# RMS-norm statistics of a three-block transformer kernel: row sums on four columns, and a scale spread back by one matmul

## The chip, the cores and the metric

One core of one Trainium2 chip runs the whole kernel as one launch. The time is device time in microseconds (us), the median of several runs. Engines are named as in the profile: PE (TensorE), ACT (ScalarE), DVE (VectorE), POOL (GpSimd), SP (SyncE, which only issues transfers here).

## The reference

512 tokens of 1024 features pass through three blocks, float32 throughout, with mixers of several kinds between the norms. What the change touches is the norm that stands ahead of every mixer and every feed-forward, 11 times on the main path:

```python
def rms_norm(t, w):
    tf = t.astype(jnp.float32)
    y = tf * lax.rsqrt(jnp.mean(tf * tf, axis=-1, keepdims=True) + NORM_EPS)
    return (y * w.astype(jnp.float32)).astype(t.dtype)

def modulate(h, shift, scale):
    return h * (1.0 + scale[:, None, :]) + shift[:, None, :]
```

The norm is followed by a product with a weight matrix. In the blocks where the kernel splits float32 operands into a rounded part ("hi") and a rest ("lo"), that product is hi·hi + hi·lo + lo·hi in the fp32r type.

## The kernel before

**Layout.** Features lie on the 128 partitions, tokens along the free axis: the residual `X(k)` and the norm's output `H(k)` are eight tiles, k = 0..7, of 128 x 512. A sum over features is therefore a sum over partitions and over the eight tiles.

**Order.** Each engine runs one program written out by hand, and they meet only through semaphores. A PE stage fills PSUM banks of a ring of four (`proj` for projections, `mix` for everything else); a key's place in the list of `mixing_keys` gives its bank. `Steps.done` makes an engine wait for its own instruction before it goes on.

**A norm.** `norm(r)`, r = 0..10, exists once for each engine. ACT squares X(k) into scratch tiles (`squares_at(r)`), each as soon as the residual of tile k is there. PE sums them with a 128x128 matrix of ones in `sum_squares` (L771), eight float32 products of 512 columns, which leaves the sum of each token on all partitions. ACT takes the root of the 128x512 result (`root`), DVE its reciprocal (`inverse`, L1682), and DVE then writes H(k) from X(k) and this factor. In the norms of `MODULATED` (0, 1, 2, 3, 9, 10) DVE multiplies by the factor only, and ACT applies gain and shift in one Identity over H(k). In those of `PLAIN` (4 to 8) DVE applies gain and factor in one instruction (L1656) and no shift exists. In `SPLIT_NORMS` ACT then rounds H(k) to hi (`round_h`), and DVE makes lo from H(k) and hi, after it has written all eight H(k).

**What follows.** Norms 1, 2, 3, 4, 5, 7 and 10 (`SPLIT_UP`) are followed by `first_pair`: PE makes two output tiles t = 0, 1 at once, for each k four products with hi of the norm (L683, L684) and, after all k, the products with lo (L689), first all of t = 0, then all of t = 1. The first two chunks of the next weight matrix are rounded by ACT (`round_chunk`) and DVE (`rest_chunk`) inside the norm. Chunk 2 goes into the buffer of chunk 0, so ACT rounds it when tile t = 0 is complete. Norm 9 is followed by projections of the context (`ck`, L648, then `cv`, L762) that don't use it, then by `rk`.

**What goes ahead.** `NORM_AFTER` names the stage ahead of norms 1 to 8. Where that is one of the four feed-forward down projections (`dn0` to `dn3`), the stage's own weight chunks, three for each output tile, are rounded by ACT in `round_down`, which stands ahead of `norm(r)`, and DVE makes their rest in `residual`. Norm 10 comes after `post_norm`, norm 0 first of all, after DVE has reduced the first rows of the modulation matrix.

Of the kernel before, what the change touches and what calls it, by code (L numbers as in the profile page):

```python
# [19 lines left out]
F32 = mybir.dt.float32  # L20
F32R = mybir.dt.float32r
I32 = mybir.dt.int32
ALU = mybir.AluOpType
# [186 lines left out]
def mixing_keys():  # L210

    k = [("ss", 0)]
# [16 lines left out]
    k += [("ss", 1), ("ss", 2)]  # L229
# [5 lines left out]
    k += [("ss", 3), ("ss", 4)]  # L235
# [6 lines left out]
    k += [("ss", 5), ("ss", 6), *(("dw", t) for t in range(KD)), ("lnm", 0), ("lnv", 0), ("ss", 7), ("ss", 8), ("ssc", 0), ("ss", 9)]  # L242
# [5 lines left out]
    k += [("ssy", 0), ("ss", 10), ("ssy", 1)]  # L248
# [29 lines left out]
class Chip:  # L278


    def __init__(self, nc, ctx, dram):
# [26 lines left out]
        self.small = sb("small", [P, 160])  # L308
# [10 lines left out]
        with ExitStack() as mlstm:  # L319
# [19 lines left out]
            "cond_ready", "pos_ready", "trig_ready", "ada_used", "ada_copied", "ada_first", "mod_ready", "sq_ready", "xn_ready", "h_ready",  # L339
# [138 lines left out]
PLAIN = {4: ("norm_mix_2", 0), 5: ("norm_ffn_2", 0), 6: ("norm_mix_2", 8), 7: ("norm_ffn_2", 8), 8: ("norm_final_2", 0)}  # L478
SQ0, RSTD = 44, 54

# [147 lines left out]
def tensor_program(nc, pe, c):  # L628
# [44 lines left out]
    def first_pair(name, r, lo):  # L673
# [100 lines left out]
    def norm(r):  # L774
        sum_squares(("ss", r), lambda k: (s["sq_ready"], 8 * r + k + 1), lambda k: T(squares_at(r) + k), KD)
# [366 lines left out]
def scalar_program(nc, act, c):  # L1142
# [17 lines left out]
    def round_h(r, k):  # L1160

        n = 8 * SPLIT_NORMS.index(r) + k + 1
        act.wait_ge(s["h_raw"], n)
        st.done(f(c.norm_hi(r, k), H(k), ACT.Copy), s["h_rounded"])
# [19 lines left out]
    def round_down(layer):  # L1184

        for n in range(SPLIT_RING, 3 * KD):
            round_chunk(f"dn{layer}", n)

    def norm(r):

        for k in range(KD):
            if r == 0:
                act.wait_ge(s["x_loaded"], 16)
            elif r in NORM_AFTER:
                act.wait_ge(*proj.emptied((NORM_AFTER[r], k)))
            else:
                act.wait_ge(s["x_ready"], 8 * (r - 9) + k + 1)
            st.done(f(T(squares_at(r) + k), X(k), ACT.Square), s["sq_ready"])
            if r in SPLIT_UP and k == KD - 2:

                up = SPLIT_UP[r]
                for n in range(SPLIT_RING):
                    round_chunk(up, n)
        root(("ss", r), T(RSTD), D)
        if r in MODULATED:
            use, layer, part, ready = MODULATED[r]
            act.wait_ge(s["mod_ready"], ready)
            for k in range(KD):
                act.wait_ge(s["xn_ready"], 8 * list(MODULATED).index(r) + k + 1)
                ins = f(H(k), H(k), ACT.Identity, scale=c.g(use, k), bias=c.m(layer, part, k))  # L1210
                ins.then_inc(s["h_raw"] if r in SPLIT_NORMS else s["h_ready"], 1)
                if r in SPLIT_NORMS:
                    round_h(r, k)
# [96 lines left out]
    def swiglu(layer):  # L1310
# [12 lines left out]
        round_down(layer)  # L1323
# [106 lines left out]
    def conv_ffn(layer):  # L1430
# [21 lines left out]
        round_down(layer)  # L1452
# [189 lines left out]
def vector_program(nc, dve, c):  # L1642
# [40 lines left out]

    def norm(r):
        if r in SPLIT_UP:
            for n in range(SPLIT_RING):
                rest_chunk(SPLIT_UP[r], n)
        inverse(("ss", r), T(RSTD))
        for k in range(KD):
            if r in MODULATED:  # L1690
                st.done(tt(H(k), X(k), T(RSTD), ALU.mult), s["xn_ready"])
            else:
                name, at = PLAIN[r]
                out = X(k) if r == 8 else H(k)
                ins = stt(out, X(k), c.v(name, at + k), T(RSTD), ALU.mult, ALU.mult)
                if r == 8:
                    st.done(ins, s["x_ready"])
                elif r in SPLIT_NORMS:
                    ins.then_inc(s["h_raw"], 1)
                else:  # L1700
                    ins.then_inc(s["h_ready"], 1)
                    dve.wait_ge(s["h_ready"], h_count(r, k))
        if r in SPLIT_NORMS:
            for k in range(KD):
                dve.wait_ge(s["h_rounded"], 8 * SPLIT_NORMS.index(r) + k + 1)
                tt(c.norm_lo(r, k), H(k), c.norm_hi(r, k).bitcast(F32), ALU.subtract).then_inc(s["h_ready"], 1)
# [23 lines left out]
    def residual(stage, gate=None, bias=None):  # L1730

        for k in range(KD):
# [670 lines left out]
```

## Time and profile before

| | us |
|---|---|
| median of 3 runs (lowest to highest) | 3945.15 (3940.18 to 3945.87) |
| the profiled execution's own time | 3940.18 |
| its span | 3938.5 |
| PE busy | 3498.3 (89% of the span) |
| DVE busy | 1952.3 (50%) |
| ACT busy | 1136.8 (29%) |
| mean granted PE clock | 0.942 |

PE is the busiest engine, but its idle time is what the other engines can shorten. In the rows below, times are us from the span's start; what stands in brackets at the end of a row is how long the engine sat idle ahead of it, and who ended that.

### The profile page before, as it was taken

The numbers are of one execution on the slowest core, as the hardware profiler recorded it, in microseconds if no ns is written. First come the engines' busy times: TensorE is split into PE (matmuls) and PEld (weight loads), VectorE is DVE, ScalarE is ACT, GpSimd is POOL, SyncE is SP. The second block draws the span as 40 slices with busy tenths as digits, with TensorE's granted clock in tenths as the row PEclk, the third lists the DMA queues.
The fourth block names the chain that finished last, engine by engine and source line by source line (L and its number), as shares of the span: only waits on it lengthen the run. The fifth ranks groups of instructions, "written<-read, shape, count | busy, mean of one in ns | idle before, by whom it ended". The sixth has DMA issues, their size and how long they took to land. (4 is left out here: it accounts for less than half of the span.)

```text
span 3938.5 us, 36809 instructions
## 1 busy us (share of the span) xinstructions
PE 3498.3 (89%) x12950; PEld 2448.4 (62%) x12950; DVE 1952.3 (50%) x2639; ACT 1136.8 (29%) x1457; POOL 111.8 (3%) x204
## 2 busy tenths in 40 slices
PE   4998789998689999965999999899997959998998
PEld 1444368886448877732588844378875725746886
DVE  5757255626438854334466259366523342316523
ACT  1211233324522213321344210244324222213221
POOL 0000000100000000000000030000000000000000
PEclk9897899999899999977999999899998979999999
DMA  5332146632025532300233311123332202222332
GB/s 210 103 117 70 32 133 192 194 118 64 22 64 193 191 121 84 94 11 7 79 95 99 93 53 54 38 86 97 95 112 75 86 11 74 86 69 75 96 97 73
DMA packets 100410, 360.90 MB, mean 92 GB/s; under 512 B 11152, under 2 KB 11168, under 8 KB 100064
## 3 DMA queue, kind: packets, MB, share of 16 engines
q1 hardware_dynamic: 77936, 276.07, 22.8%
q0 software_dynamic: 20080, 75.27, 6.0%
q10 hardware_dynamic: 2304, 8.39, 0.5%
q8 instruction: 53, 0.87, 0.1%
q14 instruction: 37, 0.30, 0.0%
HBM read 357.59 MB, written 2.10 MB: 91 GB/s over the span
## 5 line engine op out<-in xcount | busy, mean ns | idle before, releaser
L1648 DVE TENSOR_TENSOR weight_lo<-weight_ring,weight_hi 128x1024 fp32r<-128x1024 f32 (+1 forms) x422 | 508.0, 1206 | 1019.5 <-ACT weight_hi L1147 1015.5
L1147 ACT ACTIVATE weight_hi<-weight_ring 128x1024 fp32r<-128x1024 f32 (+1 forms) x422 | 440.2, 1044 | 1396.6 <-PE proj_banks L711 1058.1
L711 PE MATMUL proj_banks<-h_lo,weight_hi 128*128 128x512 f32 x1584 | 616.7, 389 | 0.0
L711 PE MATMUL proj_banks<-h_hi,weight_hi 128*128 128x512 f32 x1344 | 523.8, 390 | 8.8 <-DVE weight_lo L1648 8.8
L711 PE MATMUL proj_banks<-h_hi,weight_lo 128*128 128x512 f32 x1344 | 523.6, 390 | 0.0
L711 PEld LDWEIGHTS proj_banks<-h_lo,weight_hi 128*128 128x128 f32 x1584 | 297.8, 188 | 62.1
L711 PEld LDWEIGHTS proj_banks<-h_hi,weight_hi 128*128 128x128 f32 x1344 | 252.7, 188 | 62.3 <-issue 10.4
L711 PEld LDWEIGHTS proj_banks<-h_hi,weight_lo 128*128 128x128 f32 x1344 | 252.6, 188 | 52.7
L711 PE MATMUL proj_banks<-mid_hi,weight_hi 128*128 128x512 f32 x704 | 275.4, 391 | 7.3 <-DVE weight_lo L1648 7.3
L648 PE MATMUL proj_banks<-h_tiles,weight_ring 128*128 128x512 f32 x592 | 264.5, 605 | 13.8 <-ACT h_tiles L1147 7.3
L711 PE MATMUL proj_banks<-mid_lo,weight_hi 128*128 128x512 f32 x704 | 274.9, 390 | 0.0
L711 PE MATMUL proj_banks<-mid_hi,weight_lo 128*128 128x512 f32 x704 | 274.8, 390 | 0.0
L1147 ACT ACT_TABLE_LOAD x125 | 160.4, 1283 | 349.5 <-PE proj_banks L711 109.7
L668 PE MATMUL proj_banks<-h_tiles,weight_ring 128*128 128x512 f32 x512 | 225.7, 603 | 17.4 <-ACT h_tiles L1147 10.0
L1682 DVE RECIPROCAL scratch<-scratch 128x512 f32<-128x512 f32 (+1 forms) x39 | 129.2, 3312 | 218.7 <-ACT scratch L1147 218.6
L771 PE MATMUL mix_banks<-scratch,squares 128*128 128x512 f32 (+1 forms) x256 | 130.6, 664 | 113.8 <-ACT scratch L1147 109.2
L648 PEld LDWEIGHTS proj_banks<-h_tiles,weight_ring 128*128 128x128 f32 x592 | 114.9, 195 | 160.8 <-issue 158.2
L668 PEld LDWEIGHTS proj_banks<-h_tiles,weight_ring 128*128 128x128 f32 x512 | 98.9, 194 | 143.7 <-issue 141.9
L1147 ACT ACTIVATE scratch<-proj_banks 128x512 f32<-128x512 f32 (+1 forms) x186 | 105.0, 575 | 271.7 <-PE proj_banks L648 119.9
L1656 DVE SCALAR_TENSOR_TENSOR scratch<-proj_banks,vectors,scratch 128x511 f32<-128x511 f32 (+3 forms) x208 | 155.3, 747 | 26.8 <-ACT scratch L1147 13.3
L771 PEld LDWEIGHTS mix_banks<-scratch,squares 128*128 128x128 f32 x256 | 54.6, 220 | 180.8 <-issue 159.4
L1648 DVE TENSOR_TENSOR scratch<-scratch 128x512 f32<-128x512 f32 (+7 forms) x171 | 120.4, 704 | 87.0 <-ACT scratch L1147 45.4
(299 smaller groups left out, 5055.7 us busy)
## 6 DMA issues: line engine op xcount, KB each, us to landing
weight_ring<-in_w_up SPq DMA_DIRECT2D x176, 512.0 KB, 3.7
ada_ring<-in_ada POOLq DMA_DIRECT2D x96, 512.0 KB, 4.0
weight_ring<-in_w_dn SPq DMA_DIRECT2D x64, 512.0 KB, 3.5
weight_ring<-in_w_br SPq DMA_DIRECT2D x32, 512.0 KB, 3.7
weight_ring<-in_w_upr SPq DMA_DIRECT2D x32, 512.0 KB, 3.6
weight_ring<-in_w_dnr SPq DMA_DIRECT2D x32, 512.0 KB, 3.6
scratch<-in_ada POOLq DMA_DIRECT2D x24, 512.0 KB, 4.3
weight_ring<-in_w_dn SPq DMA_DIRECT2D x32, 384.0 KB, 3.2
```

The costliest lines, as they stand in the source:

```text
L648: last = mm(bank[:, 0:n], c.slot(chunk)[:, i * P:(i + 1) * P], rhs(k), start=k == 0, stop=k == sum(per) - 1)
L668: last = mm(proj.banks[:, u % RING, :], c.slot(ch)[:, n * P:(n + 1) * P], rhs(k), start=k == 0, stop=k == kt - 1)
L711: last = mm(proj.banks[:, u % RING, :], stationary(split0 + n)[:, w], moving(k), start=k + m == 0, stop=k == kt - 1 and m == 2)
L771: last = mm(bank[:, 0:n], c.square("ones"), tile(k), start=k == 0, stop=k == count - 1)
L1147: return nc.scalar.activation(out, in_, func, **kw)
L1648: return v.tensor_tensor(out, a, b, op)
L1656: return v.scalar_tensor_tensor(out=out, in0=a, scalar=x, in1=b, op0=op0, op1=op1)
L1682: st.link(v.reciprocal(rt, rt))
```

## The change

- **Statistics.** DVE adds squares 1 to 6 to square 0 (`sum_up`), one 128x512 add each; behind a `NORM_AFTER` stage this is spread over `residual`, otherwise it stands at the start of `norm`. PE then takes the squares as the stationary operand, four blocks of 128 tokens, against 16 columns of ones: four small products for the sum of squares 0 to 6, four more for square 7. The sum of each token now lies on its own partition, in four columns (`sum of block j` at column 16·j).
- **Root and reciprocal** are taken on 128x4. An extra 128x1 Sqrt on ACT after square 6 stands ahead of them.
- **Spread.** DVE multiplies the identity matrix by the four columns (four diagonal blocks, 128x512), and one product of ones with them puts the factor on all partitions, in a new bank ("bc", r), which stays in PSUM and is read from there.
- **Scale folded.** In the modulated norms DVE writes X·gain·factor, and ACT adds the shift while it rounds to hi; lo is made from H, shift and hi in one DVE instruction. H itself then lacks the shift.
- **Order.** `round_down` is gone: the chunks of a down projection are rounded between the squares of the norm that follows. Chunk 1 of the next stage is rounded after the root, and its rest comes after the diagonal. In `first_pair` the lo products run with k outside and t inside.

```diff
+STD, INV = 160, 164
+SUMS = 16
@@ PE
-        for t in range(2):
-            for k in range(KD):
-                if t == 0:
-                    pe.wait_ge(s["h_ready"], h_count(r, k))
+        for k in range(KD):
+            pe.wait_ge(s["h_ready"], h_count(r, k))
+            for t in range(2):
                 last = mm(proj.bank((name, t)), c.hi(split0 + t)[:, k * P:(k + 1) * P], lo(k), start=False, stop=k == KD - 1)
-            last.then_inc(proj.full_sem, 1)
+                if k == KD - 1:
+                    last.then_inc(proj.full_sem, 1)
...
     def norm(r):
-        sum_squares(("ss", r), lambda k: (s["sq_ready"], 8 * r + k + 1), lambda k: T(squares_at(r) + k), KD)
+        bank = open_bank(mix, ("ss", r))
+        for half, (sem, n) in enumerate(((s["sq_summed"], 6 * (r + 1)), (s["sq_ready"], 8 * (r + 1)))):
+            pe.wait_ge(sem, n)
+            for j in range(NB):
+                squares = T(squares_at(r) + (KD - 1 if half else 0))
+                last = mm(bank[:, j * SUMS:(j + 1) * SUMS], squares[:, j * P:(j + 1) * P], c.square("ones")[:, 0:SUMS], start=half + j == 0, stop=half + j == NB,
+                          skip_group_check=True)
+        last.then_inc(mix.full_sem, 1)
+        bank = open_bank(mix, ("bc", r))
+        pe.wait_ge(s["rstd_ready"], r + 1)
+        mm(bank, c.square("ones"), T(RSTD), start=True, stop=True).then_inc(mix.full_sem, 1)
@@ ACT, norm(r)
-                act.wait_ge(*proj.emptied((NORM_AFTER[r], k)))
+                stage = NORM_AFTER[r]
+                if stage in SPLIT:
+                    for n in range(3 * k + SPLIT_RING, min(3 * k + 3 + SPLIT_RING, 3 * KD - 1)):
+                        round_chunk(stage, n)
+                act.wait_ge(*proj.emptied((stage, k)))
...
-            if r in SPLIT_UP and k == KD - 2:
-                up = SPLIT_UP[r]
-                for n in range(SPLIT_RING):
-                    round_chunk(up, n)
-        root(("ss", r), T(RSTD), D)
+            if k == KD - 2:
+                st.link(f(c.small[:, STD:STD + 1], eps, ACT.Sqrt))
+                if NORM_AFTER.get(r) in SPLIT:
+                    round_chunk(NORM_AFTER[r], 3 * KD - 1)
+                if r in SPLIT_UP:
+                    round_chunk(SPLIT_UP[r], 0)
+        act.wait_ge(*mix.filled(("ss", r)))
+        ins = f(c.small[:, STD:STD + NB], mix.bank(("ss", r))[:, 0:NB * SUMS:SUMS], ACT.Sqrt, scale=1.0 / D, bias=eps)
+        ins.then_inc(mix.emptied(("ss", r))[0], 1)
+        if r in SPLIT_UP:
+            round_chunk(SPLIT_UP[r], 1)
...
-                ins = f(H(k), H(k), ACT.Identity, scale=c.g(use, k), bias=c.m(layer, part, k))
-                ins.then_inc(s["h_raw"] if r in SPLIT_NORMS else s["h_ready"], 1)
                 if r in SPLIT_NORMS:
-                    round_h(r, k)
+                    st.done(f(c.norm_hi(r, k), H(k), ACT.Identity, bias=c.m(layer, part, k)), s["h_rounded"])
+                else:
+                    f(H(k), H(k), ACT.Identity, bias=c.m(layer, part, k)).then_inc(s["h_ready"], 1)
@@ DVE
+    def sum_up(r, k):
+        total = T(squares_at(r))
+        dve.wait_ge(s["sq_ready"], 8 * r + k + 1)
+        st.done(tt(total, total, T(squares_at(r) + k), ALU.add), s["sq_summed"])
+
     def norm(r):
+        if r not in NORM_AFTER:
+            for k in range(1, KD - 1):
+                sum_up(r, k)
         if r in SPLIT_UP:
-            for n in range(SPLIT_RING):
-                rest_chunk(SPLIT_UP[r], n)
-        inverse(("ss", r), T(RSTD))
+            rest_chunk(SPLIT_UP[r], 0)
+        dve.wait_ge(*mix.emptied(("ss", r)))
+        st.link(v.reciprocal(small[:, INV:INV + NB], small[:, STD:STD + NB]))
+        st.done(tt(T(RSTD).rearrange("p (n c) -> p n c", c=P), c.square("ident").unsqueeze(1).broadcast_to([P, NB, P]),
+                   small[:, INV:INV + NB].unsqueeze(2).broadcast_to([P, NB, P]), ALU.mult), s["rstd_ready"])
+        if r in SPLIT_UP:
+            rest_chunk(SPLIT_UP[r], 1)
+        dve.wait_ge(*mix.filled(("bc", r)))
+        rstd = mix.bank(("bc", r))
         for k in range(KD):
             if r in MODULATED:
-                st.done(tt(H(k), X(k), T(RSTD), ALU.mult), s["xn_ready"])
+                ins = stt(H(k), X(k), c.g(MODULATED[r][0], k), rstd, ALU.mult, ALU.mult)
+                st.done(ins, s["xn_ready"])
...
@@ DVE, residual(stage), ahead of the wait for PE's tile k
+            if k >= 2:
+                sum_up(after, k - 1)
```

The order of instructions shows it at two places. First PE, norm 1 (behind the projection `abo`, ahead of the first pair of `up0`). Before:

```order
L668 MATMUL proj_banks<-h_tiles,weight_ring 128x512 x7
L657 REGISTER_ALU
L657 COMPARE_AND_BRANCH
L771 MATMUL mix_banks<-scratch,squares 128x512 [waits sq_ready,mix_empty2]
L771 MATMUL mix_banks<-scratch,squares 128x512 [waits sq_ready] x7
L683 MATMUL proj_banks<-h_hi,weight_hi 128x512 [waits w_split,proj_empty2,h_rounded]
```

And now:

```order
L674 MATMUL proj_banks<-h_tiles,weight_ring 128x512 x7
L663 REGISTER_ALU
L663 COMPARE_AND_BRANCH
L787 MATMUL mix_banks<-squares,scratch 128x16 [waits sq_summed,mix_empty3]
L787 MATMUL mix_banks<-squares,scratch 128x16 x3
L787 MATMUL mix_banks<-squares,scratch 128x16 [waits sq_ready]
L787 MATMUL mix_banks<-squares,scratch 128x16 x3
L792 MATMUL mix_banks<-scratch,squares 128x512 [waits rstd_ready,mix_empty0]
L689 MATMUL proj_banks<-h_hi,weight_hi 128x512 [waits w_split,proj_empty2,h_rounded]
```

Eight wide products have become eight narrow ones and one wide one, and that one waits for DVE's diagonal. ("squares" in these names is also the tensor that holds the constant square matrices, ones and identity among them; the squared tiles are in "scratch".)

Second DVE at the same norm, from the last residual on. Before:

```order
L1656 SCALAR_TENSOR_TENSOR x_tiles<-proj_banks,mod,x_tiles 128x512 [waits proj_full,proj_empty0]
L1648 TENSOR_TENSOR weight_lo<-weight_ring,weight_hi 128x1024 [waits w_rounded,proj_empty1]
L1648 TENSOR_TENSOR weight_lo<-weight_ring,weight_hi 128x1024 [waits w_rounded]
L1682 RECIPROCAL scratch<-scratch 128x512 [waits mix_empty2]
L1648 TENSOR_TENSOR h_tiles<-x_tiles,scratch 128x512 [waits dve_chain]
L1648 TENSOR_TENSOR h_tiles<-x_tiles,scratch 128x512 [waits xn_ready] x7
L1648 TENSOR_TENSOR h_lo<-h_tiles,h_hi 128x512 [waits h_rounded,xn_ready]
```

And now:

```order
L1667 TENSOR_TENSOR scratch<-scratch 128x512 [waits sq_ready,proj_empty0]
L1675 SCALAR_TENSOR_TENSOR x_tiles<-proj_banks,mod,x_tiles 128x512 [waits proj_full,sq_summed]
L1667 TENSOR_TENSOR weight_lo<-weight_ring,weight_hi 128x1024 [waits w_rounded,proj_empty1]
L1716 RECIPROCAL small<-small 128x4 [waits mix_empty3]
L1667 TENSOR_TENSOR scratch<-squares,small 128x512 [waits dve_chain]
L1667 TENSOR_TENSOR weight_lo<-weight_ring,weight_hi 128x1024 [waits w_rounded,rstd_ready]
L1675 SCALAR_TENSOR_TENSOR h_tiles<-x_tiles,gain,mix_banks 128x512 [waits mix_full]
L1675 SCALAR_TENSOR_TENSOR h_tiles<-x_tiles,gain,mix_banks 128x512 [waits xn_ready] x7
L1675 SCALAR_TENSOR_TENSOR h_lo<-h_tiles,mod,h_hi 128x512 [waits xn_ready,h_rounded]
```

An add of squares stands ahead of each residual, the wide reciprocal is a narrow one with the diagonal behind it, and the rest of chunk 1 lies between the diagonal and the first H(k).

## Rows read from the trace of the kernel before

**Rows 1.** Timeline around norm 1: start, us, engine, line, operation, tiles, count

```profile
508.39 7.03 PE L771 MATMUL mix_banks<-scratch,squares 128*128 128x512 f32 x16
508.66 0.75 DVE L1656 SCALAR_TENSOR_TENSOR x_tiles<-proj_banks,mod,x_tiles 128x512 f32<-128x512 f32 x1 [6.12 <-PE proj_banks L668]
509.45 0.63 ACT L1147 ACTIVATE scratch<-x_tiles 128x512 f32<-128x512 f32 x1 [4.14 <-DVE x_tiles L1656]
...
515.50 1.28 ACT L1147 ACT_TABLE_LOAD   x1 [5.42 <-PE mix_banks L771]
...
517.52 3.35 DVE L1682 RECIPROCAL scratch<-scratch 128x512 f32<-128x512 f32 x1 [5.71 <-ACT scratch L1147]
...
523.25 0.79 PE L683 MATMUL proj_banks<-h_hi,weight_hi 128*128 128x512 f32 x1 [7.82 <-ACT h_hi L1147]
...
534.88 3.82 PE L689 MATMUL proj_banks<-h_lo,weight_hi 128*128 128x512 f32 x16
...
540.75 0.47 PE L711 MATMUL proj_banks<-h_hi,weight_hi 128*128 128x512 f32 x1 [2.05 <-DVE weight_lo L1648]
```

**Rows 2.** Timeline, first product behind norms 4, 5, 6; norm 4's lo products

```profile
1551.40 0.80 PE L683 MATMUL proj_banks<-h_hi,weight_hi 128*128 128x512 f32 x1 [7.01 <-ACT h_hi L1147]
...
1560.19 3.79 PE L689 MATMUL proj_banks<-m_lo,weight_hi 128*128 128x512 f32 x16
...
1922.83 0.79 PE L683 MATMUL proj_banks<-h_hi,weight_hi 128*128 128x512 f32 x1 [5.73 <-ACT h_hi L1147]
...
2299.49 6.13 PE L648 MATMUL proj_banks<-h_tiles,weight_ring 128*128 128x512 f32 x7 [6.47 <-DVE h_tiles L1656]
```

**Rows 3.** Groups by line, and the instructions on the tensor small

```profile
L811 PE MATMUL proj_banks<-small_weights,h_tiles 128*128 128x8 f32 x64 | 11.5, 324 | 0.0
L1648 DVE TENSOR_TENSOR scratch<-scratch 128x512 f32<-128x512 f32 x130 | 90.0, 692 | 72.0 <-ACT small L1147 32.3 <-ACT scratch L1147 31.5
L1147 ACT ACTIVATE small<-small,others x2: 300/304/308, 2969.3 to 3158.2; 128x8 f32<-128x8 f32 x1, 128x16 f32<-128x16 f32 x1
```

**Rows 4.** One wide product with ones: in the chain that ended last, and the timeline

```profile
3555.97 1.14 PE mix_banks L771 x2
374.74 2.07 PE L883 MATMUL mix_banks<-scratch,squares 128*128 128x512 f32 x2
```

**Rows 5.** Windows, attention stretch: us, busy of each engine (instructions), PEclk

```profile
392.00:424.00 32.00, 15.36 (x48) 9.98 (x48) 12.55 (x46) 10.96 (x34) 0.00 (x0) 0.50 0.00 0
```

**Rows 6.** Timeline behind the first pair of norm 3

```profile
1177.70 0.47 PE L711 MATMUL proj_banks<-h_hi,weight_hi 128*128 128x512 f32 x1 [2.67 <-DVE weight_lo L1648]
```

**Rows 7.** Timeline in dn0, tile 6: residual, and rounding of the last chunk

```profile
877.34 0.75 DVE L1656 SCALAR_TENSOR_TENSOR x_tiles<-proj_banks,mod,x_tiles 128x512 f32<-128x512 f32 x1
...
880.55 0.85 ACT L1147 ACTIVATE weight_hi<-weight_ring 128x768 fp32r<-128x768 f32 x1 [4.38 <-PE proj_banks L711]
```

**Rows 8.** Timeline around norm 0

```profile
59.55 0.17 DVE L1656 SCALAR_TENSOR_TENSOR gain<-mod,vectors 128x8 f32<-128x8 f32 x1
...
67.72 2.90 PE L648 MATMUL proj_banks<-h_tiles,weight_ring 128*128 128x512 f32 x3 [7.32 <-ACT h_tiles L1147]
```

**Rows 9.** Timeline around norm 9, PE: sum of squares, ck, cv

```profile
2970.45 9.03 PE L771 MATMUL mix_banks<-scratch,squares 128*128 128x512 f32 x16 [12.21 <-ACT scratch L1147]
2979.31 13.98 PE L648 MATMUL proj_banks<-scratch,weight_ring 128*128 128x256 f32 x64
2998.43 4.83 PE L762 MATMUL proj_banks<-weight_ring,scratch 128*128 128x512 f32 x7 [5.14 <-ACT scratch L1147]
```

**Rows 10.** Timeline around norm 10, and its first pair

```profile
3553.46 0.69 DVE L1648 TENSOR_TENSOR x_tiles<-x_tiles,scratch 128x512 f32<-128x512 f32 x1
...
3563.64 0.79 PE L683 MATMUL proj_banks<-late_rounded,weight_hi 128*128 128x512 f32 x1 [6.54 <-ACT late_rounded L1147]
...
3575.25 3.79 PE L689 MATMUL proj_banks<-h_lo,weight_hi 128*128 128x512 f32 x16
...
3579.82 0.47 PE L711 MATMUL proj_banks<-late_rounded,weight_hi 128*128 128x512 f32 x1 [0.77 <-DVE weight_lo L1648]
```

More of the change, by code:

```diff
@@ L210, in mixing_keys @@
 def mixing_keys():
-    k = [("ss", 0)]
+    k = [("ss", 0), ("bc", 0)]
     k += [("rot_i", t) for t in range(5)]
@@ L234, in mixing_keys @@
         k += [("sb", h - 2)] if h >= 2 else []
-    k += [("ss", 3), ("ss", 4)]
+    k += [("ss", 3), ("bc", 3), ("ss", 4), ("bc", 4)]
     k += [("acol", 0)]
@@ L241, in mixing_keys @@
         k += [("mn", h, 0), ("mn", h, 1), ("md", h), ("stat_m", h)]
-    k += [("ss", 5), ("ss", 6), *(("dw", t) for t in range(KD)), ("lnm", 0), ("lnv", 0), ("ss", 7), ("ss", 8), ("ssc", 0), ("ss", 9)]
+    k += [("ss", 5), ("bc", 5), ("ss", 6), ("bc", 6), *(("dw", t) for t in range(KD)), ("lnm", 0), ("lnv", 0), ("ss", 7), ("bc", 7), ("ss", 8), ("bc", 8), ("ssc", 0)]
+    k += [("ss", 9), ("bc", 9)]
     k += [("rot_r", t) for t in range(8)]
@@ L307, in __init__ @@
         self.acc = sb("ada_acc", [P, 8])
-        self.small = sb("small", [P, 160])
+        self.small = sb("small", [P, 192])
         with ExitStack() as mixing:
@@ L1182, in round_ahead @@
         st_round(f(c.hi(split), c.slot(chunk), ACT.Copy))
-    def round_down(layer):
-        for n in range(SPLIT_RING, 3 * KD):
-            round_chunk(f"dn{layer}", n)
     def norm(r):
@@ L1694, in norm @@
                 out = X(k) if r == 8 else H(k)
-                ins = stt(out, X(k), c.v(name, at + k), T(RSTD), ALU.mult, ALU.mult)
+                ins = stt(out, X(k), c.v(name, at + k), rstd, ALU.mult, ALU.mult)
                 if r == 8:
@@ L1698, in norm @@
                 elif r in SPLIT_NORMS:
-                    ins.then_inc(s["h_raw"], 1)
+                    st.done(ins, s["h_raw"])
                 else:
@@ L1702, in norm @@
                     dve.wait_ge(s["h_ready"], h_count(r, k))
+        dve.sem_inc(*mix_release(mix, ("bc", r)))
         if r in SPLIT_NORMS:
@@ L1705, in norm @@
                 dve.wait_ge(s["h_rounded"], 8 * SPLIT_NORMS.index(r) + k + 1)
-                tt(c.norm_lo(r, k), H(k), c.norm_hi(r, k).bitcast(F32), ALU.subtract).then_inc(s["h_ready"], 1)
+                hi = c.norm_hi(r, k).bitcast(F32)
+                if r in MODULATED:
+                    use, layer, part, _ = MODULATED[r]
+                    ins = stt(c.norm_lo(r, k), H(k), c.m(layer, part, k), hi, ALU.add, ALU.subtract)
+                else:
+                    ins = tt(c.norm_lo(r, k), H(k), hi, ALU.subtract)
+                ins.then_inc(s["h_ready"], 1)
                 dve.wait_ge(s["h_ready"], h_count(r, k))
@@ L1730, in residual @@
     def residual(stage, gate=None, bias=None):
+        after = [r for r in NORM_AFTER if NORM_AFTER[r] == stage][0]
         for k in range(KD):
```

12 lines of the change are left out of this document (5 added, 7 removed).

## The prediction, made before the run

> **What bounds the kernel.** PE is busy for 3498.3 of 3938.5 us, so what can be won is its idle time and work that only it does. I read the timeline at the eleven norms. There every engine waits for every other, and PE can't start the next projection early.
>
> Norm 1 shows it [rows 1]. Call T the end of the projection ahead, 508.39. PE then sums squares for 7.03 us, although the last residual (0.75) and the last square (0.63) are there at T + 1.7. An ACT table load (1.28), the root and a reciprocal of 3.35 follow, then DVE's product and ACT's two steps. The first product of the pair starts at 523.25, T + 14.86, after 7.82 us idle. From its start to the end of the lo products (534.88 + 16 x 0.2275 = 538.52) the pair takes 15.27 us. 2.05 us of idle follow.
>
> Norms 2 and 3 repeat this. In the others T is the start of the first product less its idle time less 7.03: T + 14.04 at norm 4 (norm 7 is alike), T + 12.76 at norm 5, T + 13.50 at norm 6 [rows 2].
>
> **The new chain behind T**, step by step, with 0.03 to 0.1 us between engines as in the gaps of [rows 1]:
> - Residual and last square end at T + 1.69 as before. The sum of squares 0 to 6 is there by then, and PE's first four narrow products fit under these two steps.
> - Four narrow products for square 7. The nearest row is a 128x8 product with a 128x128 stationary: 64 records in 11.5 us, two records to a product [rows 3], 0.36 each. Four cost 1.44, and 0.15 for the start: T + 3.3. Bounds: 1.4, and 2.7 if each record cost the row's 324 ns.
> - ACT's root on 128x4: 0.30 as the small row with a constant operand [rows 3], T + 3.7. Its table load is gone from the chain, since the extra Sqrt takes it after square 6, when ACT waits for PE's tile 7.
> - Reciprocal of four columns: at most the same 0.30, I take 0.17. The diagonal is a 128x512 TENSOR_TENSOR, 0.69 [rows 3]: T + 4.6.
> - One wide product with ones: 1.14 at the full clock, 2.07 at 1.2 GHz [rows 4]. I take 1.5: T + 6.2.
> - DVE's first H(k) out of PSUM: 0.75, the price of the residual, which reads PSUM too [rows 1]. T + 7.05. ACT rounds it, 0.63 to 0.8: T + 7.8.
>
> So norms 1, 2 and 3 gain 14.86 - 7.8 = 7.05. Norms 4 and 7 gain 14.04 - 7.75 = 6.3. Norm 5 gains 12.76 - 7.7 = 5.1, as it had no table load on its path. Norm 6 has no rounding step and gains 13.50 - 7.0 = 6.5.
>
> **The first pair.** In norms 1, 2, 3 and 10 ACT had two instructions for each k and paced it, 15.27 us. Norm 4 had one, and its pair took 1560.19 + 3.64 - 1551.40 = 12.43 [rows 2], as PE's own work. Now all are of that kind. I take 13.0, as the start falls into the low clock for longer elsewhere: 2.3 won at each of the four. DVE writes eight H(k) at about 0.78, then eight lo at 0.76, so the last lo is there about 12.4 us behind the wide product, T + 18.6; PE wants it at T + 20.3. It stays hidden by 1.7.
>
> With t inside, tile t = 0 completes at the end of the lo products rather than seven products ahead of it, 7 x 0.2275 = 1.6 us. ACT's rounding of chunk 2 waits for it, DVE's rest waits for ACT, and PE for both (the 2.05 in [rows 1]). So 1.6 us is given back after seven pairs. Norm 3 is the exception: there DVE and ACT were late behind the pair with other work of the modulation (idle 2.67, [rows 6]), which now fits under the faster chain. I count its 1.6 as nothing and 0.2 more won.
>
> **Down projections.** ACT now rounds chunks between squares, and DVE's add (0.69) goes ahead of the residual. In dn0 the residual of tile 6 starts at 877.34 and ends at 878.09. With the add it ends at 878.85, and the square at 879.5. The next rounding could not start before 880.55 anyway [rows 7], so 1.0 us of cover is left on each tile. At tile 6 table load and Sqrt (1.5) come between and round the last chunk 0.5 later. It is rounded and split 1.8 us later, and PE reaches this chunk, the last 18 products of tile 7, 18 x 0.2275 = 4.1 us ahead of T = 889.9, at 885.8. I cost all this at nothing.
>
> **Norms that lose.** In norm 0 the squares were ready long before DVE finished its rows at 59.72 [rows 8]. Now six adds (6 x 0.72) start only there, 64.1, both halves of narrow products run behind them (3.0), then root, reciprocal, diagonal (1.3), wide product at the low clock (2.0), and two steps (1.6): 72.0 instead of 67.72, +4.3. DVE itself ends 4.9 later. I take +4.5.
>
> Norm 10: DVE ends the update of X at 3554.15 [rows 10]. Adds to 3558.5, then 3.0 + 1.3 + 2.0 + 1.6 give 3566.4 for the first product instead of 3563.64, +2.8. The pair wins 15.25 - 13.0 = 2.2 and gives back 1.6: +2.2.
>
> Norms 8 and 9 belong together. The statistics of norm 8 are ready 3.7 earlier, and with them the context's transfer, squares and norm. But PE now stands in norm 9 until the wide product is issued, where before it went on to ck at 2979.31 [rows 9]. From 2970.45 - 0.7 - 3.7 = 2966.0: seven squares 4.6, table load and Sqrt 1.5, last square 0.6, then 1.6 + 0.4 + 0.9 + 2.0 = 2977.6. ck starts 1.7 earlier but at the low clock, so it ends where it did. Behind it cv waited 5.14 us for ACT, which was at the sixteen operations of norm 9. Now there are eight and they start earlier, so cv comes at about 2995 instead of 2998.43: -3.4. Bounds: 0 (the wait stays) and -5.
>
> **Sum.** Norm 1: -7.05 - 2.3 + 1.6 = -7.75, and norm 2 the same. Norm 3: -9.6. Norms 4 and 7: -6.3 + 1.6 = -4.7 each. Norm 5: -3.5. Norm 6: -6.5. Norms 8 and 9: -3.4. Norm 10: +2.2. Norm 0: +4.5. Together -41.2. The profiled execution took 3940.18, which gives 3899. It is the lowest of the three runs, 5 us under the median of 3945.15, and the new median may as well lie 5 us above: 3904. I say 3900.
>
> **The clock.** In the attention stretch PE is busy for 15.36 of 32 us, in short products with idle stretches between, and the granted clock stays at 0.50, which is 1.2 GHz [rows 5]. The new chain leaves PE about 4 us of narrow work in 7.8, so I keep a low clock at the start of each pair, as before. The Trainium skill (TensorE: Matmul & The Clock Gate, "HAM oscillation") blames the low clock on long idle gaps of PE between groups of products, and the new chain has only short ones, of about 1.5 us each. By this the clock would stay high, which the attention row speaks against.
>
> The table load: the row shows 1.28 us, and the root starts right behind it, so its removal is worth 1.28 a norm. The Trainium skill (ScalarE: Activation LUTs, "What ACT_TABLE_LOAD costs") adds a drain of about 1.38, 2.66 in all. By its figure the seven norms would win some 10 us more. The trace shows no such drain here, and the sum stays with the row.
>
> **Rivals.**
> - *As forecast*: 3900, own range 3889 to 3911. Chance 0.66.
> - *The clock stays high through the new chain.* The pair of 48 products then takes 48 x 0.2275 = 10.9 instead of 13.0, and lo on DVE allows about 11.3: 1.7 won at six pairs (not norm 10, where PE idles long), 0.35 at each of seven wide products, 2.5 at norm 6. That is -15, 3885. For it: the gaps are short. Against: [rows 5]. Chance 0.13.
> - *Handovers and narrow products cost more.* Nine handovers replace six. If the four narrow products cost 2.7 and each root and reciprocal 0.3 more, that is 1.9 for each of ten norms: +19, 3919. For it: the 324 ns of the row are the length of a record. Against: 64 of them fit in 11.5 us. Chance 0.14.
> - *Slower: the down projections stall.* If DVE's add waits for ACT's square of the tile before, and ACT's next rounding waits for the residual behind that add, PE waits for a chunk at each of 7 tiles in 4 stages. It decides against the change when a tile loses 41.2 / 28 = 1.5 us, that is when the residual ends 1.0 + 1.5 = 2.5 us later than I work out, and PE has no store of chunks (the ring holds two). At 2 us a tile it is +15, 3955. For it: two buffers only. Against: the 1.0 of cover and 3 us more before PE wants the chunk. Chance 0.04.
> - *No change*: PE's idle time behind T is hidden anyway, or norms 0, 9 and 10 lose more than I see, 3940. Against: the first product waits for ACT's hi in every norm. Chance 0.03.
>
> **Chances.** Range 3881 to 3920, from the second case to the third. About 0.2% (8 us) is what a measurement of this kernel can tell from no change. Faster 0.94, same 0.03, slower 0.03.
>
> **What the profile will show.** Right: behind norm 1 PE's first product comes 7.8 us after T, the wide product at about T + 4.7, and the reciprocal of 3.35 us is gone from the norms; the pair takes 12.4 to 13.2 us in all seven, and the idle time behind it is 3.6 where a table load stands there, 2.4 where not; norm 0 starts its projection near 72. Wrong: idle time of PE inside dn0 to dn3, narrow products of over 2 us for four, PEclk at 1.0 at the start of a pair, or cv still at the same distance behind ck. I would be most wrong if the down projections stalled.

## The result: 0.36% slower, and the profile after

The changed kernel takes 3954.34 us (median of ten runs, 3949.25 to 3961.64). The kernel before takes 3939.62 on the same chips (ten runs, 3939.03 to 3945.87). The ratio is 1.0036, with a 95% interval from 1.0027 to 1.0046. So it is slower by 15 us, where 3900 was forecast. The profiled execution took 3956.17, with a span of 3954.4 against 3938.5. One of the ten runs of e5 below took 5349.91 us, at a granted clock of 0.64, and is left out of its median and ratio.

Norm 1 shows what the norms themselves did. This is the timeline of the changed kernel: start and duration in us, engine, line, operation, tiles, count, and in brackets the idle time ahead. T, the end of the projection, is now 509.95.

```profile
510.22 0.75 DVE L1675 SCALAR_TENSOR_TENSOR x_tiles<-proj_banks,mod,x_tiles 128x512 f32<-128x512 f32 x1 [4.60 <-PE proj_banks L674]
...
511.00 0.63 ACT L1164 ACTIVATE scratch<-x_tiles 128x512 f32<-128x512 f32 x1 [3.57 <-DVE x_tiles L1675]
...
511.69 1.06 PE L787 MATMUL mix_banks<-squares,scratch 128*128 128x16 f32 x8 [0.78 <-ACT scratch L1164]
...
512.85 0.26 ACT L1164 ACTIVATE small<-mix_banks,others 128x4 f32<-128x4 f32 x1 [1.22 <-PE mix_banks L787]
...
513.15 0.18 DVE L1716 RECIPROCAL small<-small 128x4 f32<-128x4 f32 x1 [0.92 <-ACT small L1164]
513.36 0.69 DVE L1667 TENSOR_TENSOR scratch<-squares,small 128x512 f32<-128x512 f32 x1
...
514.20 1.10 PE L792 MATMUL mix_banks<-scratch,squares 128*128 128x512 f32 x2 [1.44 <-DVE scratch L1667]
515.33 3.10 DVE L1675 SCALAR_TENSOR_TENSOR h_tiles<-x_tiles,gain,mix_banks 128x512 f32<-128x512 f32 x4
516.17 2.29 ACT L1164 ACTIVATE h_hi<-h_tiles,mod 128x512 fp32r<-128x512 f32 x3 [2.11 <-DVE h_tiles L1675]
516.95 0.80 PE L689 MATMUL proj_banks<-h_hi,weight_hi 128*128 128x512 f32 x1 [1.66 <-ACT h_hi L1164]
...
534.30 0.47 PE L717 MATMUL proj_banks<-h_hi,weight_hi 128*128 128x512 f32 x1 [3.63 <-DVE weight_lo L1667]
```

The chain has the links that were forecast, and its first product comes at T + 7.00 instead of T + 14.86 [rows 1]; the forecast had T + 7.8. The idle time behind the pair is 3.63, as forecast (3.6). The table load has left this chain.

Yet all this lies 1.6 us later than before at the start, and at norm 2, T is 893.38 where it was 889.87, although norm 1 had put the kernel 6.45 ahead (534.30 against 540.75). The loss lies in the long stretches between norms. The windows of TensorE over two of them show it: us, busy of PE and PEld, then DVE, ACT and POOL (instructions in brackets), PEclk, share of DMA, GB/s. Kernel before:

```profile
2000.00:2100.00 100.00, 100.00 (x443) 82.84 (x442) 66.39 (x84) 48.86 (x56) 0.00 (x0) 1.00 0.32 96
3700.00:3800.00 100.00, 100.00 (x443) 82.83 (x442) 39.35 (x47) 26.65 (x32) 0.00 (x0) 1.00 0.32 95
```

Changed kernel, the same stretches:

```profile
2000.00:2100.00 100.00, 100.00 (x432) 81.09 (x431) 64.73 (x83) 47.90 (x54) 0.00 (x0) 1.00 0.29 94
3700.00:3800.00 100.00, 100.00 (x433) 81.18 (x432) 41.00 (x51) 25.50 (x32) 0.00 (x0) 1.00 0.30 95
```

PE is busy for all of both, at the full granted clock in both, and still it starts 432 products where it started 443. Busy share and clock say nothing here; the count does. The groups by line say it again, with the mean duration of one product in ns. Before:

```profile
L711 PE MATMUL proj_banks<-h_lo,weight_hi 128*128 128x512 f32 x1584 | 616.7, 389 | 0.0
L711 PE MATMUL proj_banks<-mid_hi,weight_hi 128*128 128x512 f32 x704 | 275.4, 391 | 7.3 <-DVE weight_lo L1648 7.3
```

After:

```profile
L717 PE MATMUL proj_banks<-h_lo,weight_hi 128*128 128x512 f32 x1584 | 626.9, 396 | 0.0
L717 PE MATMUL proj_banks<-mid_hi,weight_hi 128*128 128x512 f32 x704 | 279.2, 397 | 6.7 <-DVE weight_lo L1667 6.7
L654 PE MATMUL proj_banks<-h_tiles,weight_ring 128*128 128x512 f32 x592 | 264.1, 605 | 2.8 <-ACT h_tiles L1164 1.8 <-DVE h_tiles L1675 1.0
```

The rounded (fp32r) products of this line are all longer by 5 to 7 ns; the plain fp32 products of L654 took 605 ns before too. The idle times in the last column are no larger in the down projections (6.7 against 7.3 ahead of the mid products). The distance between the starts of two consecutive rounded products, over all pairs under 0.32 us apart (some 9,700 in each trace; single distances jump by a few ns, so only means count), is **227.0 ns before, 232.6 ns after**. There are 9,936 rounded products by the counts of their groups, and 9,936 x 5.6 is 56 us. That is the size of the miss, 3954 against 3900.

Nothing in the order of the program touches these products. What the change does touch is the table of tensors: `small` grew from 160 to 192 columns for STD and INV, and everything allocated behind it moved up by 128 bytes in each partition.

### The profile page after: what moved, and what is told of

Same layout as the page of the kernel before. It is cut to its first block and busy times, and to the rows that moved or that the text cites. A ratio compares the mean times of both kernels' runs of the same rounds, so it can differ in the third digit from the quotient of the medians.

```text
span 3954.4 us, 36962 instructions
## 1 busy us (share of the span) xinstructions
PE 3517.1 (89%) x12972; PEld 2454.5 (62%) x12972; DVE 1977.5 (50%) x2716; ACT 1105.7 (28%) x1428; POOL 112.8 (3%) x204
## 5 line engine op out<-in xcount | busy, mean ns | idle before, releaser
L717 PE MATMUL proj_banks<-h_lo,weight_hi 128*128 128x512 f32 x1584 | 626.9, 396 | 0.0
L717 PE MATMUL proj_banks<-h_hi,weight_hi 128*128 128x512 f32 x1344 | 533.5, 397 | 13.2 <-DVE weight_lo L1667 13.2
L717 PE MATMUL proj_banks<-h_hi,weight_lo 128*128 128x512 f32 x1344 | 532.5, 396 | 0.0
L654 PE MATMUL proj_banks<-h_tiles,weight_ring 128*128 128x512 f32 x592 | 264.1, 605 | 2.8 <-ACT h_tiles L1164 1.8
L1667 DVE TENSOR_TENSOR scratch<-scratch 128x512 f32<-128x512 f32 (+5 forms) x237 | 165.9, 700 | 107.0 <-ACT scratch L1164 65.1
L654 PEld LDWEIGHTS proj_banks<-h_tiles,weight_ring 128*128 128x128 f32 x592 | 114.8, 194 | 150.6 <-issue 148.3
L1701 DVE RECIPROCAL scratch<-scratch 128x512 f32<-128x512 f32 (+1 forms) x28 | 92.3, 3295 | 159.9 <-ACT scratch L1164 159.8
L1675 DVE SCALAR_TENSOR_TENSOR scratch<-scratch,vectors 128x512 f32<-128x512 f32 x212 | 159.4, 752 | 7.5
L717 PEld LDWEIGHTS proj_banks<-mid_hi,weight_hi 128*128 128x128 f32 x704 | 133.2, 189 | 39.0 <-DVE weight_lo L1667 7.6
```

The lines of the kernel that those rows point to most:

```text
L654: last = mm(bank[:, 0:n], c.slot(chunk)[:, i * P:(i + 1) * P], rhs(k), start=k == 0, stop=k == sum(per) - 1)
L717: last = mm(proj.banks[:, u % RING, :], stationary(split0 + n)[:, w], moving(k), start=k + m == 0, stop=k == kt - 1 and m == 2)
L1667: return v.tensor_tensor(out, a, b, op)
L1675: return v.scalar_tensor_tensor(out=out, in0=a, scalar=x, in1=b, op0=op0, op1=op1)
L1701: st.link(v.reciprocal(rt, rt))
```

## The experiments

In all of them "mean distance" is that of the starts of rounded products, counted as above. Times are medians. The runs were spread over three chips, and "before" was timed beside each on the same chip (3938.49 to 3939.50); ratios and intervals are against that.

### e1: the old addresses under the changed program

```diff
-        self.small = sb("small", [P, 192])
+        self.small = sb("small", [P, 160])
-STD, INV = 160, 164
+STD, INV = 144, 148
```

> The changed kernel with its eight columns for root and reciprocal put into free columns (144 to 151) of the tensor small, which keeps its old width of 160: every tensor allocated behind it (h_tiles, scratch, h_hi, h_lo, mid_hi, mid_lo and others) lies at the address of the kernel before, where the change moved them up by 128 bytes a partition. Theory A, addresses: the starts of rounded products (L717 and its like, some 9,900 of them) go from a mean of 232.4 ns apart back to 226.7, and 9,900 x 5.7 ns = 56 us come off 3954: 3898. Theory B, the place of TensorE's program in its instruction memory (22 products more, semaphore waits more): nothing moves, 3954 and 232.4 ns. Theory C, the numbers of the semaphores (three new names ahead of the others): 3954 as well.

Measured: **3900.91** (ratio to before 0.9899, interval 0.9884 to 0.9914), mean distance 226.9 ns. Theory A gets 3898 and is met; B and C fall. Of the miss of 54 us, 53 are the width of one small tensor. PE's count in the first stretch is that of before again:

```profile
2000.00:2100.00 100.00, 100.00 (x443) 82.84 (x442) 65.26 (x83) 49.68 (x57) 0.00 (x0) 1.00 0.32 97
```

### e2: the new addresses under the old program

```diff
-        self.small = sb("small", [P, 160])
+        self.small = sb("small", [P, 192])
```

> The kernel before with the tensor small 192 columns wide and nothing else: the addresses of the changed kernel under the program of the kernel before. Theory A: each rounded product takes 5.7 ns more, 3940 + 56 = 3996. Theories B and C: 3940, spacing 226.7 ns.

Measured: **3992.24** (1.0135, 1.0120 to 1.0151), mean distance 232.5 ns. The kernel before loses 53 us by 32 columns that nobody uses.

### e3: the numbers of the semaphores

The edit puts `"sq_summed", "std_ready", "rstd_ready",` into the list of semaphores of the kernel before, and nothing else.

> The kernel before with the three new semaphore names in the list at the place where the change puts them, unused: the numbers of all later semaphores move by three. Theory C: 3996 and 232.4 ns. Theories A and B: 3940 and 226.7 ns.

Measured: 3938.36 (0.9996, 0.9987 to 1.0005). Theory C is out on this side too.

### e4: the first pair in its old order

```diff
-        for k in range(KD):
-            pe.wait_ge(s["h_ready"], h_count(r, k))
-            for t in range(2):
+        for t in range(2):
+            for k in range(KD):
+                if t == 0:
+                    pe.wait_ge(s["h_ready"], h_count(r, k))
```

> The changed kernel with the lo products of the first pair in the old order, tile t outside k (the rest as changed). The forecast's term: tile 0 completes seven products earlier, 1.6 us off the wait behind each of seven pairs, 11 us in all, 3943. Rival: the wait behind the pair is set by ACT's copy of tile 1 or by the rounding and splitting of the third chunk alone, and nothing is won: 3954. Theory B adds that the few instructions that move may change the spacing of the products (232.4 ns) in either direction, up to 56 us; by A and C the spacing stays.

Measured: 3943.70 (1.0008, 0.9999 to 1.0017), 10.6 us under the changed kernel; the expectation was 11. The mean distance stays at 232.6 ns. The idle times behind the seven pairs, where the term was looked for, add up to 20.4 us in the changed kernel and to 9.3 in e4. The row behind norm 5 shows it; here it is in the changed kernel:

```profile
1933.63 0.47 PE L717 MATMUL proj_banks<-h_hi,weight_hi 128*128 128x512 f32 x1 [3.62 <-DVE weight_lo L1667]
```

and here in e7, where the order is the old one too:

```profile
1901.53 0.47 PE L717 MATMUL proj_banks<-h_hi,weight_hi 128*128 128x512 f32 x1 [2.05 <-DVE weight_lo L1667]
```

That 11.1 and 10.6 agree so well is in part luck. The profiled executions differ by 13.0, and not only behind the pairs: T of norm 1, ahead of the first pair, stands 4.7 later in e4, the four loops behind norms 1, 3, 5 and 7 are together 7.8 shorter in it, and the loop behind norm 10 is 1.6 longer (more on that one below e15).

### e5, e6, e9: which distance is it?

e5 makes `small` 224 wide. e6 adds 32 unused columns ahead of everything. e9 does that and makes `small` 192 wide:

```diff
+        self.pad = sb("pad", [P, 32])
         self.x = sb("x_tiles", [P, KD * S])
```

> The kernel before with small 224 columns wide: h_lo, mid_hi, h_hi and the rest move up by 256 bytes (e2: 128). Theory M, parity of the address: a rounded product is longer when its moving operand begins at an even multiple of 128 bytes in the partition (e2: 199680), as before when at an odd one (before: 199552). Here it begins at an odd one, 199808: 3940 and 226.9 ns between starts. Theory R, distance: what counts is whether the distance between moving operand (h, mid) and weights (weight_hi, weight_lo) is an odd multiple of 128 bytes (e2); here it is an even one again: 3940. Theory P, only the very distance of before (768 modulo 2048) is good: 3992.

> The kernel before with 32 unused columns ahead of x_tiles: everything moves up by 128 bytes, the weights too, so moving operands begin at an even multiple (199680, as in e2) and all distances are those of before. Theory M: 3992, 232.5 ns. Theories R and P: 3940, 226.9 ns.

> The kernel before with both: 32 columns ahead of x_tiles and small 192 wide. Weights move up by 128 bytes, h and mid by 256: moving operands begin at an odd multiple (199808), and the distance to the weights is an odd multiple, as in e2. Theory M: 3940, 226.9 ns. Theories R and P: 3992, 232.5 ns.

Measured: e5 3938.22 (1.0006, 0.9996 to 1.0016), 227.0 ns. e6 3940.11 (1.0005, 0.9996 to 1.0015), 226.9 ns. e9 3991.64 (1.0133, 1.0116 to 1.0150), 232.7 ns. Theory M falls twice: in e6 the moving operands have the absolute addresses of e2, and it is fast; in e9 they begin at an odd multiple, and it is slow. P falls by e5. R, a distance between tensors, is left, and e9 against e6 is its measure: 51.5 us.

### e7: both repairs

> The changed kernel with both repairs: small 160 wide (3901 alone) and the lo products of the first pair with the tile outside k (10.6 us alone, from 3954 to 3944). If the two add, 3890. Rival: part of the 10.6 came from the layout of the program and does not come again: 3901.

Measured: **3886.28** (0.9874, 0.9857 to 0.9890). From e1 that is 14.6 us, more than the 10.6 of e4 alone. So the two add at the least: the idle times behind the seven pairs fall from 20.9 us in e1 to 10.4. The 4 us beyond are not the edit's: in the profiled executions T of norm 1, ahead of the first pair, already stands at 507.44 in e7 and at 512.78 in e1, whose programs are the same up to there. The long mixing stretch ahead of norm 1 takes some us more or less from one execution to the next.

### e10: the old statistics where nothing is won by the new

Norms 0 and 10 go back to `sum_squares`, `root` and `inverse` on 512 columns, on the kernel of e7:

```diff
+OLD_SUMS = (0, 10)
...
+        if r in OLD_SUMS:
+            sum_squares(("ss", r), lambda k: (s["sq_ready"], 8 * r + k + 1), lambda k: T(squares_at(r) + k), KD)
+            return
```

> The kernel of e7 (3886) with the statistics of norms 0 and 10 as before (eight wide products, root and reciprocal on 512 columns, no adds and no second product), while the folded scale stays. In e1 the first projection after norm 0 started 5.4 us later than before (73.1 against 67.7), and the first pair of norm 10 13.2 us behind the last update of X, before 9.5. If these are the adds, the narrow products and the wide product behind them, the first gives back 5.4 and the second 4.4 (8.8 behind the update, since ACT has one step less): 3876. Rival: other work of the start and of norm 10 ends last anyway, 3886.

Measured: **3878.38** (0.9847, 0.9830 to 0.9863), 7.9 us under e7 (on another chip; the kernel before differs by 0.4 between the two) and 1.5% under the kernel before. Norm 10's first product comes 9.07 us behind the last update of X (3494.11 to 3503.18), forecast 8.8, before 9.49 [rows 10]. This is the best version that I ran.

### e11, e13: half a step and a quarter

`small` is 176 and 168 columns wide, in the kernel before.

> The kernel before with small 176 wide: h and mid move up by 64 bytes against the weights. If the parity of 128-byte steps is all that counts and a step holds for its whole width, half a step gives either 3940 or 3992; if each product is slowed by the share of its reads that fall into the wrong step, the half: 3966.

> As e11 with 168: a move of 32 bytes. By shares a quarter of the 52 us: 3953. By whole steps 3940 or 3992.

Measured: e11 3963.50 (1.0058, 1.0041 to 1.0075), 229.6 ns, near the half. e13 4002.02 (1.0157, 1.0140 to 1.0174), 233.3 ns: a move of 32 bytes costs more than one of 128. Neither shares nor steps of 128 bytes explain both. That expectation failed.

### e12, e15, e14, e16: which tensors?

e12 puts 32 unused columns between `weight_hi` and `weight_lo`. e15 does so and widens `small` to 192. e16 puts 64 columns there. e14 puts 32 between `weight_ring` and `weight_hi`:

```diff
         self.w_hi = sb("weight_hi", [P, SPLIT_RING * SLOT], F32R)
+        self.pad = sb("pad", [P, 32])
         self.w_lo = sb("weight_lo", [P, SPLIT_RING * SLOT], F32R)
```

> The kernel before with 32 unused columns between weight_hi and weight_lo: weight_lo, h and mid move up by 128 bytes, weight_hi stays. Two of three products use weight_hi. Theory R1, a product is longer when its moving operand and its own weights stand at an odd distance: hi x weight_hi and lo x weight_hi are long, hi x weight_lo short, 2/3 of 52 us: 3975. Theory R2, it is longer when the weights that are loaded under it, those of the next product, stand at an odd distance: lo x weight_hi (weight_lo loads under it) is short and the two others long, 3975 as well; the starts tell which. Theory R3, the long ones are due to what ScalarE, VectorE and the DMAs do in weight_ring and weight_hi meanwhile, and since ring to h is odd as in e2: 3992.

Measured: 3996.04 (1.0142, 1.0125 to 1.0159), 233.2 ns. R1 and R2 want two thirds of the products long, and all are. R3 gets the time, but e14 was made to test it:

> The kernel before with 32 unused columns between weight_ring and weight_hi: weight_hi, weight_lo, h and mid move up by 128 bytes together, weight_ring stays. TensorE's own operands in a rounded product keep their distances. If these alone count: 3940 and 226.9 ns. If the distance to weight_ring counts, where the DMAs write and ScalarE and VectorE read (R3): 3992.

Measured: 3939.40 (1.0000, 0.9991 to 1.0010), 227.0 ns. The distance to `weight_ring`, where the DMAs write and ScalarE and VectorE read, costs nothing. R3 falls. The end of the program in e2 says the same. The last rounding by VectorE starts at 3959.47 and ends at 3960.70; after it no engine but PE works, and the products go on at the long distance. From 3962.12 to 3968.17 there are 26 distances, 232.7 ns in the mean. VectorE's row, and the first and the last of those products:

```profile
3959.47 1.23 DVE L1648 TENSOR_TENSOR weight_lo<-weight_ring,weight_hi 128x1024 fp32r<-128x1024 f32 x1 [4.29 <-ACT weight_hi L1147]
...
3962.12 0.39 PE L711 MATMUL proj_banks<-relu_hi,weight_lo 128*128 128x512 f32 x1
...
3968.17 0.39 PE L711 MATMUL proj_banks<-late_rounded,weight_hi 128*128 128x512 f32 x1
```

So it is between TensorE's own operands.

> The kernel before with 32 unused columns between weight_hi and weight_lo, and small 192 wide: weight_lo moves up by 128 bytes, h and mid by 256, so only weight_lo stands at an odd distance to the two others. If a product is long where moving operand and its own weights are at an odd distance, one of three is: 3957. If the distance of weight_hi to weight_lo makes all long, as e12 could be read: 3996. If it is that of moving operand to weight_hi (odd in e2, e9 and e12): 3940.

Measured: 3975.70 (1.0091, 1.0074 to 1.0108), 231.2 ns. None of the three numbers is met: it is 36 us, two thirds of e2 and e12 (53 and 57). The timeline tells which two of three, though not in one triple. These are two of e15's (PE only):

```profile
2100.43 0.39 PE L712 MATMUL proj_banks<-h_hi,weight_hi 128*128 128x512 f32 x1
2100.66 0.40 PE L712 MATMUL proj_banks<-h_lo,weight_hi 128*128 128x512 f32 x1
2100.89 0.40 PE L712 MATMUL proj_banks<-h_hi,weight_lo 128*128 128x512 f32 x1
2101.12 0.39 PE L712 MATMUL proj_banks<-h_hi,weight_hi 128*128 128x512 f32 x1
...
2101.82 0.39 PE L712 MATMUL proj_banks<-h_hi,weight_hi 128*128 128x512 f32 x1
2102.04 0.40 PE L712 MATMUL proj_banks<-h_lo,weight_hi 128*128 128x512 f32 x1
```

From hi x weight_hi to the next start it is 0.23 or 0.22. Over the 265 triples between 2000 and 2200 us, with the starts in whole ns, the means are 226.6 ns from hi x weight_hi to lo x weight_hi, 232.5 from there to hi x weight_lo, 234.2 from there to the next hi x weight_hi. In e12 the same three are 232.9, 232.1 and 235.0.

Only `weight_lo` is at an odd distance in e15. The interval of the product that uses it is long, and that of the product ahead of it too, whose own operands are both even. One reading fits the loops with `h` and `mid` as moving operand in all runs that move a tensor by a multiple of 128 bytes: **an interval between two rounded products is long when, among the operands of the product and of the one behind it, moving operand and weights stand at an odd multiple of 128 bytes**. e2, e9 and e12 have this in all three, e15 in two. The changed kernel has it in two of three in upr (the loop behind norm 10), where hi lies in `late_rounded` ahead of `small`; the mean distance there, from 3600 to 3700 us, is 231.1, and 226.7 + 2/3 x 6.6 is 231.1.

But this reading, put together after the runs, does not hold everywhere. Interval by interval, that upr has 231.2, 229.6 and 232.9, where long, long and short would be due. e4 has every address of the changed kernel, and in the same stretch of upr its mean distance is 233.3 and not 231.1. PE starts fewer products in it; the changed kernel, then e4:

```profile
3600.00:3700.00 100.00, 100.00 (x435) 81.22 (x434) 53.03 (x72) 28.07 (x37) 0.00 (x0) 1.00 0.31 94
3600.00:3700.00 100.00, 100.00 (x431) 80.47 (x429) 52.32 (x71) 27.82 (x36) 0.00 (x0) 1.00 0.30 94
```

In upr of e15 the reading wants two long intervals of three, and from 3640 to 3740 us the mean is 228.9, which is one. In the products of norm 4 whose moving operand is the weights and whose stationary one is h (mv, within 1605 to 1665 us), it wants all three long in e12 and two in e15, and the means are 229.4 and 233.2. So the runs show that the relative place of the operands decides; which interval gets long, and what else counts (e4), stays open. With one trace for each kernel it is also open whether e4's upr is due to its order or to that one execution. How TensorE comes to it was not tested, nor what a distance of 32 or 64 bytes does to each product.

> The kernel before with 64 unused columns between weight_hi and weight_lo: weight_lo, h and mid move up by 256 bytes. All distances are multiples of 256 bytes. By that rule 3940 and 226.9 ns; if any other distance than that of before is bad, some 3990.

Measured: 3938.81 (0.9998, 0.9989 to 1.0008), 227.0 ns. With every distance a multiple of 256 bytes all is as before, as in e5 and e6.

## Why the prediction was wrong, step by step

**The step that failed is the sum**: "Together -41.2. The profiled execution took 3940.18, which gives 3899." It takes the work outside the eleven norms over from the old trace, and prices the wider `small` at nothing without a word. The change moved h_hi, h_lo, mid_hi and mid_lo by 128 bytes against their weights. It cost 53 us by itself (e2), and 53.4 of the changed kernel's time (3954.3 less 3900.9, e1). None of the rivals held it. The slower one, stalls in the down projections, had the right time, 3955, by a mechanism that isn't there: the whole of PE's waits on weight_lo in line 717 is 22.3 us in seven waits. Five stand behind norms 1, 3, 5, 7 and 10 (15.6), and two at the start of dn0 and dn1, 0.26 and 6.47, where the kernel before has 0.52 and 6.75. The row of the waits (us in total, times, longest) of the changed kernel:

```profile
PE proj_banks L717 <- DVE weight_lo L1667: 22.3, 7, 6.5
```

and in e7, where the 1.6 at each pair is undone:

```profile
PE proj_banks L717 <- DVE weight_lo L1667: 16.0, 7, 6.7
```

Everything else can be judged by e1, whose addresses are those of the forecast. Its profiled span is 3898.2, 40.3 us under that of before, where the sum said 41.2. From T to the first product of the loop behind the pair, e1 against before:

| norm | before | e1 | difference | forecast |
|---|---|---|---|---|
| 1 | 32.36 | 24.20 | -8.2 | -7.75 |
| 2 | 31.07 | 23.02 | -8.1 | -7.75 |
| 3 | 32.93 | 23.23 | -9.7 | -9.6 |
| 4 | 27.52 | 24.15 | -3.4 | -4.7 |
| 5 | 27.65 | 24.08 | -3.6 | -3.5 |
| 6 (to T of norm 7) | 273.75 | 265.90 | -7.9 | -6.5 |
| 7 | 29.40 | 24.13 | -5.3 | -4.7 |
| 8, 9 (T of 8 to ssy0) | 592.09 | 587.41 | -4.7 | -3.4 |
| 10 (ssy0 to the loop) | 50.32 | 53.41 | +3.1 | +2.2 |
| 0 (to T of norm 1) | 508.39 | 512.78 | +4.4 | +4.5 |

Unrounded these make -43.2; the stretches between them give back 2.9. Of this 1.6 lie in up0: at its start the granted clock is 0.56 in e1 (538.6 to 542.0 us), and eight products come 427 ns apart; in the kernel before it is 1.00 at that place.

- **The chain** was right: in the changed kernel the first product comes at T + 7.0 and 6.8 where the wide product runs at the full clock (1.10 us, norms 1 and 5), and at T + 7.9 where it runs at the low one (2.04, norms 2 and 3). The 1.5 between the two bounds was a fair mean, and 7.8 lies at the long end. The clock did not stay high through the chain in norm 2, though PE's idle stretches ahead of the wide product were only 0.78 and 1.44 us: it was granted 1.00 up to 896.2 us, and 0.50 from 897.6.
- **The first pair** was over-rated at norm 4: it got longer there, from 12.4 to 13.8 us (1525.62 to 1535.73 + 3.64), and the gain is 3.4 instead of 4.7.
- **The handovers** cost what the gaps say; that rival needed 1.9 more a norm.
- **The give-back** of 1.6 behind each pair is 11.1 in all by the idle times of e4, and 10.5 by those of e7 against e1. The sum had it at six pairs, 9.6: I had booked norm 3 at nothing, and its idle went from 2.67 [rows 6] to 2.34, where the old order would have left 1.04 (e4).
- **Norm 0** was right for the reason given, and 1 us short: in the changed kernel the adds stand in front of everything, and the first product comes 5.4 us later than before [rows 8], for +4.5. The +4.4 of the table agrees with the forecast only by chance, since the stretch behind, up to norm 1, varies by as much (T of norm 1 stands at 507.44 in e7 and 512.78 in e1). The rows:

```profile
59.67 4.32 DVE L1667 TENSOR_TENSOR scratch<-scratch 128x512 f32<-128x512 f32 x6
64.14 3.56 PE L787 MATMUL mix_banks<-squares,scratch 128*128 128x16 f32 x16 [64.14 <-DVE scratch L1667]
...
69.22 2.04 PE L792 MATMUL mix_banks<-scratch,squares 128*128 128x512 f32 x2 [1.51 <-DVE scratch L1667]
...
73.09 1.19 PE L654 MATMUL proj_banks<-h_tiles,weight_ring 128*128 128x512 f32 x1 [1.84 <-ACT h_tiles L1164]
```

- **Norms 8 and 9**: the sign and the place were right, the way partly wrong. In e1 ck starts 43.7 us behind T of norm 8, before 41.9, so it comes later and not earlier: the sum waits for DVE's adds (17.37). But cv no longer waits at all [rows 9], and follows ck at once. This is e1:

```profile
2935.51 3.56 PE L787 MATMUL mix_banks<-squares,scratch 128*128 128x16 f32 x16 [17.37 <-DVE scratch L1667]
2940.59 2.05 PE L792 MATMUL mix_banks<-scratch,squares 128*128 128x512 f32 x2 [1.51 <-DVE scratch L1667]
2942.43 15.05 PE L654 MATMUL proj_banks<-scratch,weight_ring 128*128 128x256 f32 x64
2957.31 1.02 PE L768 MATMUL proj_banks<-weight_ring,scratch 128*128 128x512 f32 x2
```

- **Down projections** cost nothing, as said: dn0 has the same wait of 0.52 us in e1 as before, and a stretch that holds up2 and dn2 and no norm takes 348.28 us in before (1937.71 to 2285.99) and in e1 (1912.11 to 2260.39), with the new order of rounding, adds and squares in it. In the changed kernel it takes 358.57 (1933.63 to 2292.20), and by e1 that is the longer products.

## What to carry to other kernels

A forecast that sums only the touched instructions assumes that the untouched ones keep their duration; where a change alters the size of any tensor, list the addresses of everything allocated behind it, and see whether the distance between a rounded product's moving operand and its weights stays a multiple of 256 bytes. Put new small columns into free room, or pad to the next 256 bytes. And look at counts of products for each 100 us, or at starts, since an engine that is 100% busy at full clock can be 2.5% slower without any other sign; a statistic that is moved off one engine should be used only where the engine that takes it over is idle (norms 0 and 10 lost by it).

## What the runs showed of the hardware that was not expected

The mean distance between two rounded 128x512 products depends on where their operands lie relative to one another in the partition: 226.9 to 227.0 ns when moving operand, weight_hi and weight_lo are multiples of 256 bytes apart (before, e1, e5, e6, e14, e16), 232.5 to 233.2 when moving operand and weight_hi are an odd multiple of 128 apart (e2, e9, e12), 231.2 when only weight_lo is (e15), 229.6 at 64 bytes and 233.3 at 32 (e11, e13). These are means over whole traces; single loops differ (upr of e4 and e15). Plain fp32 products of the same shape stay at 604 to 606 ns in before, after, e1 and e2. Absolute addresses, the distance to weight_ring and what other engines do there don't matter (e6, e14, the end of e2).

The Trainium skill (SBUF — State Buffer, "SBUF: two separate sides") gives TensorE a second, independent read port for loading weights, and lets it never wait on anyone. That other engines don't disturb it agrees with e14. If that independence held between TensorE's own two operands too, the place of the weights would not matter either; e12 and e15 show that it does, by 57 and 36 us, and the measurement decides.
